# First gate and value products of the FFN: high and low activations as one 512-column matmul over the high weights, halves added at evacuation

## The reference

```
h = rms_norm(x, norm2_w)
u = causal_dwconv(h @ w_up, ffn_conv_w, ffn_conv_b)     # w_up: 2048 x 11264, 3 taps over positions
u_gate, u_val = jnp.split(u, 2, axis=-1)                # 5632 columns each
return x + (jax.nn.silu(u_gate) * u_val) @ w_down       # w_down: 5632 x 2048
```

## Time and profile before

| | us |
|---|---|
| median of 2 runs | 1541.36 |
| lowest, highest | 1540.91, 1541.81 |
| span of the profiled execution, first to last instruction | 1537.5 |
| TensorE matmuls busy in it | 1524.5 (12,586 matmuls) |
| VectorE busy | 1136.1 |
| ScalarE busy | 778.1 |

### The profile page before, as it was taken

The page is one execution under the profiler, slowest core; times in us unless marked ns, Lnnn a source line. Parts: engine busy times, 40 slices in busy tenths (PEclk is TensorE's granted clock), DMA queues, the critical chain, the costliest instruction groups (busy, mean ns, idle before and its releaser), DMA issues. The chain is left out here.

```text
span 1537.5 us, 32072 instructions
## 1 busy us (share of the span) xinstructions
PE 1524.5 (99%) x12586; PEld 1483.7 (97%) x12586; DVE 1136.1 (74%) x1373; ACT 778.1 (51%) x930; POOL 29.8 (2%) x56
## 2 busy tenths in 40 slices
PE   9999999999999999999999999999999999999997
PEld 8999997999999999999999999999999989999997
DVE  7877777657987878788788887879854644764754
ACT  7645455545554444444444444445554643454554
POOL 0000000000000000000000000000000000000000
PEclk9999999999999999999999999999999999999999
DMA  9474556457877767677686776866465554445451
GB/s 348 171 272 161 200 177 220 146 171 273 302 282 249 288 233 273 244 249 274 235 293 229 262 272 221 300 219 217 150 247 194 196 193 162 160 159 185 154 186 58
DMA packets 85932, 339.23 MB, mean 221 GB/s; under 512 B 9680, under 2 KB 10208, under 8 KB 79328
## 3 DMA queue, kind: packets, MB, share of 16 engines
q1 hardware_dynamic: 77760, 281.05, 52.1%
q0 software_dynamic: 7232, 54.55, 10.1%
q10 hardware_dynamic: 864, 2.53, 0.4%
HBM read 335.97 MB, written 2.12 MB: 220 GB/s over the span
## 5 line engine op out<-in xcount | busy, mean ns | idle before, releaser
L683 DVE TENSOR_TENSOR wlo<-raw,whi 128x1024 fp32r<-128x1024 f32 x528 | 643.3, 1223 | 345.9 <-ACT whi L320 342.2
L320 ACT ACTIVATE whi<-raw 128x1024 fp32r<-128x1024 f32 x528 | 557.5, 1059 | 646.5 <-PE PS L1328 573.6
L1324 PE MATMUL PS<-gh,whi 128*128 128x256 f32 x3096 | 863.7, 279 | 0.7 <-DVE gl L1208 0.3
L1326 PE MATMUL PS<-gl,whi 128*128 128x256 f32 x3096 | 856.1, 277 | 0.0
L1328 PE MATMUL PS<-gh,wlo 128*128 128x256 f32 x3096 | 856.1, 277 | 0.0
L1324 PEld LDWEIGHTS PS<-gh,whi 128*128 128x128 f32 x3096 | 581.7, 188 | 5.9 <-issue 2.6
L1326 PEld LDWEIGHTS PS<-gl,whi 128*128 128x128 f32 x3096 | 581.4, 188 | 0.8
L1328 PEld LDWEIGHTS PS<-gh,wlo 128*128 128x128 f32 x3096 | 581.6, 188 | 0.0
L1324 PE MATMUL PS<-ah,whi 128*128 128x256 f32 x688 | 189.9, 276 | 0.0
L1328 PE MATMUL PS<-ah,wlo 128*128 128x256 f32 x688 | 189.9, 276 | 0.0
L1326 PE MATMUL PS<-al,whi 128*128 128x256 f32 x688 | 189.9, 276 | 0.0
(11 more groups left out here) (256 smaller groups left out, 894.6 us busy)
## 6 DMA issues: line engine op xcount, KB each, us to landing
raw<-weights SPq DMA_DIRECT2D x528, 512.0 KB, 3.6
ada_w<-w_ada POOLq DMA_DIRECT2D x48, 1024.0 KB, 5.9
EM<-rows POOLq DMA_DIRECT2D x1, 3072.0 KB, 12.4
X<-xT SPq DMA_DIRECT2D x3, 512.0 KB, 8.3
c<-const ACTq DMA_DIRECT2D x1, 1536.0 KB, 7.1
c_act<-c_rows POOLq DMA_DIRECT2D x1, 1024.0 KB, 7.0
outT<-X SPq DMA_DIRECT2D x2, 512.0 KB, 3.2
outT<-X SPq DMA_DIRECT2D x3, 256.0 KB, 2.2
```

What stands on the lines that cost most here:

```text
L320: act.activation(whi[:, j % SPLIT, :], raw[:, j, :], ACT.Copy).then_inc(s_hi, 1)
L683: dve.tensor_tensor(wlo[:, j % SPLIT, :], raw[:, j, :], whi[:, j % SPLIT, :].bitcast(F32), ALU.subtract).then_inc(s_lo, 1)
L1324: pe.matmul(out[:, t, :], whi[:, b, w], hi[:, kt, :], start=first and half == 0 and (apart or t % 2 == 0), stop=False, skip_group_check=True)
L1326: pe.matmul(out[:, t, :], whi[:, b, w], lo[:, kt, :], start=False, stop=False, skip_group_check=True)
```

## The change

For the two blocks of step 0 alone, TensorE streams both halves of the activations, `gh` and `gl` of one tile, as one moving operand of 2 x 256 = 512 columns over the high weights, into a bank of its own for each output tile: columns 0 to 255 of the bank collect the high part, 256 to 511 the low part. The low weights by `gh` go on top of the high part as before. That makes 8 matmuls of 512 columns and 8 of 256 in a unit. Four banks are used where two were (2, 3, 6, 7 and 0, 1, 4, 5). At the evacuation ScalarE copies the low parts into `UG` or `UV` (`wide_low`, two activations of 128x512, then `s_wide`); VectorE adds the high parts from PSUM to them (two operations of 128x512), waits for its own result, and multiplies by `rb` in SBUF (128x1024), then raises `s_evac`.

The sum of squares is issued after the fifth unit of the first block instead of after its eighth, ScalarE's `root` after six of the eight splits, and TensorE waits for the root (`s_root`) before the second block, which writes bank 4. `gh` and `gl` become the two halves of one array `G` at the same addresses. The other ten steps and everything else are unchanged.

```diff
-        gh, _ = place("gh", [P, DT, S], F32R)
-        at[0] += 0
-        gl, _ = place("gl", [P, DT, S], F32R)
+        G, _ = place("g", [P, 2, DT, S], F32R)
+        gh, gl = G[:, 0, :, :], G[:, 1, :, :]
...
+        def wide_tile(par, t):
+
+            return PS[:, 2 * par + (t % 2) + 4 * (t // 2), :]
+
+        def wide_half(par, k):
+
+            return [PS[:, 4 * a + 2 * par:4 * a + 2 * par + 2, S * k:S * k + S] for a in range(2)]
...
 # ScalarE
-            group(B_FF)
+            def wide_low(last, par, dst):
+
+                act.wait_ge(s_used, last + 1 + SPLIT)
+                for a, low in enumerate(wide_half(par, 1)):
+                    ins = act.activation(dst[:, 2 * a:2 * a + 2, 2:2 + S], low, ACT.Copy)
+                ins.then_inc(s_wide, 1)
+
+            for j in range(6):
+                split(B_FF, LEAD + j)
             root(1, D)
+            for j in range(6, 8):
+                split(B_FF, LEAD + j)
+            wide_low(8 * B_FF + 7, G_FF % 2, UG)
             split(B_FF + 1, LEAD)
             act.wait_ge(s_evac, G_FF + 1 + 2)
             ffn_base(0, False)
             for j in range(1, 8):
                 split(B_FF + 1, LEAD + j)
+            wide_low(8 * B_FF + 15, (G_FF + 1) % 2, UV)
...
 # VectorE
+            def wide_evac(last, grp, par, dst):
+                finished(last, grp)
+                dve.wait_ge(s_wide, grp - G_FF + 1)
+                for a, high in enumerate(wide_half(par, 0)):
+                    out = dst[:, 2 * a:2 * a + 2, 2:2 + S]
+                    ins = dve.tensor_tensor(out, high, out, ALU.add)
+                link(ins)
+                flat = dst[:, :, 2:2 + S]
+                dve.tensor_tensor(flat, flat, rb[:, :].unsqueeze(1).to_broadcast([P, 4, S]), ALU.mult).then_inc(s_evac, 1)
...
-            ffn_evac(8 * B_FF + 7, G_FF, G_FF % 2, UG)
+            wide_evac(8 * B_FF + 7, G_FF, G_FF % 2, UG)
...
-            ffn_evac(8 * B_FF + 15, G_FF + 1, (G_FF + 1) % 2, UV)
+            wide_evac(8 * B_FF + 15, G_FF + 1, (G_FF + 1) % 2, UV)
...
 # TensorE
+            def wide(blk, grp, par, need, units):
+
+                if 0 in units:
+                    pe.wait_ge(s_evac, grp + 1)
+                for u in units:
+                    pe.wait_ge(s_lo, blk * 8 + u + 1)
+                    pe.wait_ge(s_gl, need(2 * u + 1))
+                    for half in range(2):
+                        kt = 2 * u + half
+                        for t in range(4):
+                            w = slice(512 * half + P * t, 512 * half + P * t + P)
+                            pe.matmul(wide_tile(par, t), whi[:, u % SPLIT, w], G[:, :, kt, :], start=kt == 0, stop=False,
+                                      skip_group_check=True)
+                            mm = pe.matmul(wide_tile(par, t)[:, 0:S], wlo[:, u % SPLIT, w], gh[:, kt, :], start=False,
+                                           stop=kt == DT - 1, skip_group_check=True)
+                    mm.then_inc(s_used, 1)
...
-            whole(B_FF, G_FF, G_FF % 2, need_ff)
+            wide(B_FF, G_FF, G_FF % 2, need_ff, range(5))
             sum_squares(1, SQX2)
-            whole(B_FF + 1, G_FF + 1, (G_FF + 1) % 2, need_ff)
+            wide(B_FF, G_FF, G_FF % 2, need_ff, range(5, 8))
+            pe.wait_ge(s_root, 2)
+            wide(B_FF + 1, G_FF + 1, (G_FF + 1) % 2, need_ff, range(8))
```

More of the change, by code:

```diff
@@ L251, in build @@
         s_prm2 = sem("s_prm2")
+        s_wide = sem("s_wide")
         s_tile, s_part = sem("s_tile"), sem("s_part")
```

## The result

The changed kernel takes 1566.97 us (median of 2 runs, 1566.86 to 1567.09) against 1541.36: ratio 1.0172, 95% interval 1.0155 to 1.019. It is 25.6 us slower, where I had forecast 0.3 us. The profiled execution took 1567.09 us, with a span of 1565.4, 27.9 us more than the span before.

What follows compares the result with a forecast made beforehand. The prediction took TensorE's matmul stream as the bound: +0.3 us of matmuls and 0 of waits raised the 1537.5 us span to 1537.8, and the kept 3.9 us difference gave 1541.7 us, range 1539.9 to 1543.6.

Steps and rivals of the forecast that it cites:

- The bound: Whole kernel: TensorE's matmul stream sets the time; an edit counts by changing that stream or making TensorE wait.
- ScalarE's root: Before the second wide block: root done by 397.0 us, TensorE's new wait released 2.6 us early, cost 0.
- the sum of my terms: VectorE's evacuation: 0.61 + 0.69 + 0.03 + 1.14 = 2.47 us instead of 1.14, twice, with no wait for TensorE.
- ScalarE's two copies: Evacuation: copying the low halves from PSUM takes about 1.3 us, in idle time, cost 0.
- The third rival, late splits: Unit 13, behind the longer evacuation: late splits make TensorE stand 1.1 us; 1542.8 us, or 1543.9 behind both groups; chance 0.16.
- A long matmul is not cheaper than two short ones: Wide blocks: 228.9 ns for 512 columns against 226.7 ns for two of 256, dearer by 2.2 ns.
- a saved fixed part: Wide blocks, first rival: each dropped matmul saves a fixed 6.7 ns, 0.85 us in all, 1540.5 us; chance 0.18.
- the pace of the weight load: Wide blocks, second rival: weight loads pace short matmuls, wide ones escape; 14.5 us less at the extreme, 1526.9 us; chance 0.03.
- With 228.9 ns the edit costs 128 x 2.2 ns = +0.3 us: Two wide blocks: 128 pairs priced with the existing 512-column matmuls' 228.9 ns, giving +0.3 us.
- the pace does not change with what else runs: TensorE's ordinary units: 2.72 us each in both windows read, whatever the other engines do.
- the whole form of the sum: TensorE's stream: only the 16 edited units of 528 change, +0.3 us of matmuls and 0 of waits.

Runs made afterwards that it cites:

- the timed run of the two short ones: Changed kernel with each 512-column matmul issued as two of 256, timed in ten runs: 1540.05 us against 1540.38 for the kernel before.
- the grouped order: Changed kernel with each contraction tile's four wide matmuls first, then its four narrow ones; timed 1540.66 us against 1540.38 for the kernel before.
- the run with two long ones in a row: Changed kernel plus two extra 512-column float32r matmuls, result unused, behind the second wide block: 1542.35 us.
- the first experiment: Changed kernel plus TensorE's wait for its own last matmul behind the second wide block: 1540.76 us, kernel before 1539.82; timed later 1542.23 against 1540.38.
- closed banks: Changed kernel with the stop flag on the last wide matmul of each output tile, so no part of a bank stays open: 1566.72 us.
- one piece: Changed kernel with high and low activations of a tile side by side, so the wide matmul's moving operand is 512 contiguous columns: 1567.36 us.
- the short one first: Changed kernel with the short matmul ahead of the long one in each pair, start flag on the short one: 1567.96 us.
- the float32 matmul: Changed kernel plus one plain float32 matmul of 256 columns, result unused, behind the second wide block: 1566.92 us.

## Why the prediction was wrong

The bound was read rightly: TensorE's stream sets the time, and all of the loss is in it. These steps held:
- ScalarE's root was done at 397.35 us (forecast 397.0), 2.8 us before unit 7 ended (400.15, forecast 399.59), and no wait of TensorE is on record between 380 and 480 us.
- VectorE's evacuation took 2.47 us to the next start, exactly the sum of my terms. VectorE's timeline (answers to the earlier trace rows):

```profile
404.93 1.29 DVE L1090 TENSOR_TENSOR UG<-PS,UG 128x512 f32<-128x512 f32 x2
406.25 1.23 DVE L1093 TENSOR_TENSOR UG<-UG,rb 128x1024 f32<-128x1024 f32 x1
407.40 1.22 DVE L703 TENSOR_TENSOR wlo<-raw,whi 128x1024 fp32r<-128x1024 f32 x1
```

- ScalarE's two copies took 1.06 us (forecast 1.3) and lay in idle time. The third rival, late splits, did not happen; the timed run of the two short ones puts all of this at 0.
- A long matmul is not cheaper than two short ones. In the slow rhythm it costs the same (235 against 2 x 117.7). The first two rivals, a saved fixed part and the pace of the weight load, fall with that.

Two steps failed. The smaller is the term "With 228.9 ns the edit costs 128 x 2.2 ns = +0.3 us": the pair took 353 ns instead of 342, 1.4 us more than forecast for 128 of them. The 228.9 was measured where 512-column matmuls follow each other, and was used for a place where they alternate with short ones. In the grouped order it comes near: 1.387 / 4 = 347 ns for a long and a short one, which makes 0.9 us for the 16 units where I had 0.3. (A slip beside it: the range was to reach the first rival less the spread, 1540.5 - 0.9 = 1539.6, and the third rival, 1543.9; I wrote 1539.9 and 1543.6. It decides nothing here.)

The larger is the sentence that the pace does not change with what else runs, and behind it the whole form of the sum: 16 edited units times a difference, nothing for the other 512. I took 113.3 ns as the property of a 256-column matmul. It is one of two paces of the same matmul, and its row does not say when it gets which. The trace of before has both, and I did not look. TensorE in its first stage:

```profile
76.02 0.28 PE L1324 MATMUL PS<-gh,whi 128*128 128x256 f32 x1
76.14 0.28 PE L1326 MATMUL PS<-gl,whi 128*128 128x256 f32 x1
...
76.61 0.28 PE L1328 MATMUL PS<-gh,wlo 128*128 128x256 f32 x1
```

Five steps in 0.59 us, 118 ns each, with the same operands and the same kind of matmul as the earlier trace rows, 4% slower and with no wait. A group's mean hid it: the page of before gives L1326 277 ns for its 3096 matmuls with `gl`, a mixture of many with 276 and some with 281.

```profile
L1326 PE MATMUL PS<-gl,whi 128*128 128x256 f32 x3096 | 856.1, 277 | 0.0
```

The traces show two things more about the rhythms. First, the program does not fix which one a stretch gets. Sixteen steps of the same matmuls, in code that no edit touches, in the kernel before and in the run with two long ones in a row:

```profile
92.14 0.28 PE L1324 MATMUL PS<-gh,whi 128*128 128x256 f32 x1
...
94.02 0.28 PE L1326 MATMUL PS<-gl,whi 128*128 128x256 f32 x1
```

```profile
92.18 0.28 PE L1354 MATMUL PS<-g,whi 128*128 128x256 f32 x1
...
93.99 0.28 PE L1356 MATMUL PS<-g,whi 128*128 128x256 f32 x1
```

The first takes 1.88 us, 117.5 ns a step, the second 1.81 us, 113.1. Of the 14 kept profiles nine are slow in this stretch and five fast. Second, a short pause can set the rhythm anew, and to either of the two. The kernel before, in the second layer:

```profile
1107.82 0.28 PE L1326 MATMUL PS<-gl,whi 128*128 128x256 f32 x1
...
1108.62 0.28 PE L1328 MATMUL PS<-gh,wlo 128*128 128x256 f32 x1
1108.86 0.36 PE L1324 MATMUL PS<-gh,whi 128*128 128x256 f32 x1
1109.06 0.28 PE L1326 MATMUL PS<-gl,whi 128*128 128x256 f32 x1
...
1111.65 0.28 PE L1328 MATMUL PS<-gh,wlo 128*128 128x256 f32 x1
1112.01 0.36 PE L1324 MATMUL PS<-gh,whi 128*128 128x256 f32 x1
1112.20 0.28 PE L1326 MATMUL PS<-gl,whi 128*128 128x256 f32 x1
...
1113.22 0.28 PE L1326 MATMUL PS<-gl,whi 128*128 128x256 f32 x1
```

Seven steps of 114 ns, a delayed step of 0.24 us, 22 steps of 118 ns, a delayed step of 0.36 us, and nine steps of 113 ns. Other pauses leave it as it is: in the first experiment's run a step of 0.36 us at 1116.25 us has slow steps of 118 ns ahead of it and behind it.

Had I asked what could put the long FFN stream into that second rhythm, the rival would have been 264 x 0.105 = 28 us slower, and the edit, which changes the pattern of the stream right ahead of 248 units that nothing interrupts, its likely trigger.

## What to carry to other kernels

Before pricing an edit to a dense matmul stream, list the distances from start to start over the whole trace, not the mean of a group: where one kind of matmul shows two distances, the stream has more than one rhythm, and an edit can move long unchanged stretches from one to the other. Merging two 256-column matmuls into one of 512 saved no time here; if different lengths must be mixed, keep equal ones together, and leave no strict turn of long and short in front of a long uninterrupted stream. When unchanged code is slower after an edit, put one pause behind the edit: where the time comes back, the loss was in what the edit left behind and not in the edit. Where it does not come back, nothing is shown yet, since a pause can also start the slow rhythm. And time such kernels several times: a difference of 27 us can be one run's rhythm.

## What was not expected of the hardware

- A stream of 128x256 float32r matmuls with a weight load each runs at 113.3 or at 117.7 ns from start to start, at the full granted clock in both cases (2.4 GHz level, 1.00 in the windows), and keeps the one it is in over 248 units, some 6000 matmuls.
- A strict turn of 512 and 256 columns goes at 353 ns a pair and leaves the slow rhythm behind, in all six runs of kernels with the turn and nothing behind it that ended the rhythm (two of the changed kernel and one each with closed banks, one piece, the short one first and the float32 matmul). A single 512-column matmul did not, in one run, nor did groups of four and four, in eleven. An idle time of 0.47 us ended it in eleven runs and two 512-column matmuls in a row in one; one plain float32 matmul did not, in one. Other pauses in the same traces start the slow rhythm, as above.
- The slow rhythm can be caught without any long matmul. The first stage of the kernel before has it in stretches among its short interruptions, and one of the ten timed runs with two short matmuls for each long one took 1567.52 us (span 1565.9) where the other nine took 1538.62 to 1541.17; no profile of that run exists, so that it was this rhythm is only likely from its size. It is the only such run among 64 of the kernels without the turn, or with something behind it that ends the rhythm. So the turn is what makes the long loss sure here, and not the only way into it.
- In the changed kernel the granted clock fell for a moment where TensorE pauses for the norm between the layers (0.94 in the window 1123.5 to 1126 us and 0.72 in 1126 to 1131.5, 1.00 after). The slow rhythm ends at the same pause. The two do not belong together: with closed banks the rhythm ends there too, and the granted clock stays at 1.00 from 1126 to 1131.5 us; and in the run with one 512-column matmul, which has no slow rhythm to end, the clock falls at the same pause (0.62 in the window 1099 to 1103.5 us).

What in TensorE holds the rhythm stays open: the trace shows starts and modelled ends, not the state of the queue. Whether the pause works by its length, by the moment at which the stream starts again, or because the stream has run empty was not told apart. No version tried beats the kernel before: with the rhythm mended the change costs 0 to 2 us, since the stream's price is its columns, and these are the same.
